# A transformer block on one core: the retention stage in rounds with inputs made a round ahead, decay carried by v, and three wide TensorE products per round whose result nothing reads

## The reference

```python
inner = jnp.einsum('bnihd,bnjhd->bnhij', qc, kc) * decay
inner = jnp.einsum('bnhij,bnjhe->bnihe', inner, vc)
def step(state, kv_chunk):
    k_i, v_i = kv_chunk
    new_state = (jnp.einsum('bjhd,bjhe->bhde', k_i * zeta[None, :, :, None], v_i)
                 + chunk_decay[None, :, None, None] * state)
    return new_state, state
cross = jnp.einsum('bnihd,nbhde->bnihe', qc, prev_states) * xi[None, None, :, :, None]
o = (inner + cross).reshape(b, s, h, dv)
mu = jnp.mean(o32, axis=-1, keepdims=True)
var = jnp.mean(jnp.square(o32 - mu), axis=-1, keepdims=True)
o = ((o32 - mu) * lax.rsqrt(var + RET_GN_EPS)).astype(dt).reshape(b, s, RET_WIDTH)
o = o * gn_w + gn_b
return jax.nn.silu(g) * o
```

## Time and profile before

| what | value |
|---|---|
| median of 3 runs | 2777.88 us (2776.36 to 2779.82) |
| profiled execution, its own time | 2776.76 us |
| its span, first to last instruction | 2775.0 us |
| PE, PEld, DVE, ACT, POOL busy | 94%, 80%, 56%, 40%, 37% of the span |
| mean granted TensorE clock | 0.950 of full speed |
| retention units, first to last `r_at`, layer 0 | 561.5 to 630.2 us |
| start of the output projection, layer 0 | 648.7 us |

### The profile page before, as it was taken

How to read it: one execution, slowest core, us unless ns; L and a number is a source line. 1 busy time by engine, 2 the same in 40 slices (tenths; PEclk the granted TensorE clock), 3 DMA queues, 4 the chain that set the end, 5 groups by cost and what they waited for, 6 DMA issues and landing times. The chain is left out here.

```text
span 2775.0 us, 43012 instructions
## 1 busy us (share of the span) xinstructions
PE 2597.4 (94%) x12940; PEld 2228.0 (80%) x12940; DVE 1560.8 (56%) x3033; ACT 1107.1 (40%) x2567; POOL 1039.7 (37%) x1229
## 2 busy tenths in 40 slices
PE   6999988889999999999989998988998999999997
PEld 5999877767778888888879998776776888888886
DVE  4666554473455445477656765544726544545785
ACT  4444543352532232244444455434515232322444
POOL 3455522183154544301034554222812555442012
PEclk9999999958999999999999999998599999999999
DMA  5111101121223332483331101012022323335633
GB/s 173 28 36 41 30 15 37 38 84 61 103 73 110 106 110 93 148 292 96 103 107 31 34 19 39 6 37 89 32 91 76 111 84 104 110 104 207 231 95 122
DMA packets 238651, 243.06 MB, mean 88 GB/s; under 512 B 27904, under 2 KB 170752, under 8 KB 238464
## 3 DMA queue, kind: packets, MB, share of 16 engines
q1 hardware_dynamic: 238464, 240.83, 27.0%
HBM read 173.14 MB, written 67.63 MB: 87 GB/s over the span
## 5 line engine op out<-in xcount | busy, mean ns | idle before, releaser
L2319 POOL TENSOR_TENSOR fw_a_lo<-fw_a_raw,fw_a_hi 128x512 fp32r<-128x512 f32 x132 | 178.7, 1354 | 520.6 <-DVE fw_s_raw L1913 520.6
L2319 POOL TENSOR_TENSOR fw_s_lo<-fw_s_raw,fw_s_hi 128x512 fp32r<-128x512 f32 x176 | 231.4, 1327 | 54.6 <-ACT fw_s_hi L1422 54.6
L718 PE MATMUL banks<-ht_hi,da_hi 128*128 128x512 f32 x496 | 192.9, 389 | 0.0
L718 PE MATMUL banks<-ht_lo,da_hi 128*128 128x512 f32 x496 | 192.9, 389 | 0.0
L718 PE MATMUL banks<-ht_hi,da_lo 128*128 128x512 f32 x496 | 192.9, 389 | 0.0
L718 PE MATMUL banks<-w_diff_hi,ht_hi 128*128 128x384 f32 x512 | 181.2, 354 | 6.3 <-DVE ht_lo L1609 4.3
L718 PE MATMUL banks<-w_diff_hi,ht_lo 128*128 128x384 f32 x512 | 172.9, 338 | 0.0
L718 PE MATMUL banks<-w_diff_lo,ht_hi 128*128 128x384 f32 x512 | 172.8, 337 | 0.0
L2158 POOL TENSOR_TENSOR qk_rot<-rope_a,rope_b 128x512 f32<-128x512 f32 x64 | 82.6, 1291 | 211.7 <-DVE rope_b L1638 211.7
L1666 DVE TENSOR_REDUCE stats<-banks 128x1 f32<-128x1024 f32 (+3 forms) x192 | 138.3, 747 | 29.8 <-PE banks L919 24.9
L718 PE MATMUL banks<-h_t_hi,fw_s_hi 128*128 128x512 f32 x352 | 139.9, 398 | 12.2 <-DVE h_t_lo L1917 8.2
(11 more groups left out here) (351 smaller groups left out, 7647.5 us busy)
## 6 DMA issues: line engine op xcount, KB each, us to landing
da_raw<-act_scratch SPq DMA_DIRECT2D x154, 256.0 KB, 2.7
fw_a_raw<-in_w_gate_dram SPq DMA_DIRECT2D x88, 256.0 KB, 3.0
act_scratch<-act_s SPq DMA_DIRECT2D x66, 256.0 KB, 3.0
w_diff_raw<-in_w_in_dram SPq DMA_DIRECT2D x24, 512.0 KB, 6.0
fw_a<-in_w_up_dram SPq DMA_DIRECT2D x44, 256.0 KB, 3.2
fw_a_raw<-in_w_up_dram SPq DMA_DIRECT2D x44, 256.0 KB, 2.9
act_scratch<-act_zero SPq DMA_DIRECT2D x44, 256.0 KB, 2.4
act_scratch<-act_one SPq DMA_DIRECT2D x44, 256.0 KB, 2.8
```

Of the source, the lines that this page charges most:

```text
L718: mm = pe.matmul(bank, lhsT, rhs, start=first and i == 0, stop=last and i == len(pairs) - 1, skip_group_check=resumes)
L2319: pool.tensor_tensor(w[1][:], w[2][:], w[0][:].bitcast(F32), ALU.subtract).then_inc(S["f_lo"], 1)
```

## The change

- The decays move onto v and the normalization. v is multiplied by gamma^-(j+1)/8 on VectorE right before its unit's rotation, in the MLA stage; `decay` becomes a 0/1 triangle (`causal`, 64 KB in place of 256 KB); the common factor left on a row drops out of the normalization, whose eps is scaled (`xz[:, p, 2:4]`). So `r_xzt`, its four scalings and the third transpose go. The state that is handed on is scaled by chunk decay where it is rounded.
- All engines loop over `RET_STEPS`, with v and the gate made two steps ahead. VectorE has the sum of the output first in a step (`ret_take`) and makes the rest of the state, which GpSimd made.
- The normalization moves from VectorE to ScalarE as scale and bias (`ret_normed`, with `ret_offset` on VectorE); root and finish on GpSimd take two units at once.
- `keep_clock` issues a product of 512 columns into a bank that nothing reads, after the transposes, after inner and after the output of every step: 48 per layer.
- The splits of the first half of the output weights stand in steps 4, 7, 10 and 13. `load_out(1)` waits for the finish of the fifth pair of units (`r_mx`, 5). The transposes of `mixed_rows` take the six column blocks of the attention heads first, of both halves of the rows, then the two of the retention.

```diff
-    xi = np.exp((pos[:, None] + 1.0) * log_gamma[None, :])
-    zeta = np.exp((P - 1.0 - pos)[:, None] * log_gamma[None, :]) * RET_DIM ** -0.5
+    age = (pos[:, None] + 1.0) * log_gamma[None, :].astype(np.float64)
     for p in range(RET_PAIRS):
-        c[:, C_XZ + 4 * p:C_XZ + 4 * p + 2] = xi[:, 2 * p:2 * p + 2]
-        c[:, C_XZ + 4 * p + 2:C_XZ + 4 * p + 4] = zeta[:, 2 * p:2 * p + 2]
...
+        RET_STEPS = range(RET_UNITS + 8)
+        ROUND_OUT = {4: 0, 7: 1, 10: 2, 13: 3}
...
-                arrives(decay[:], decay_dram.rearrange("p (a n) -> p a n", a=RET_PAIRS), "ret_in")
+                arrives(causal[:], causal_dram, "ret_in")
...
-                sp.wait_ge(S["r_xz"], L * PER["r_xz"] + T + 2)
-                sp.wait_ge(S["r_vlo"], L * PER["r_vlo"] + T + 2)
+                sp.wait_ge(S["r_mx"], L * PER["r_mx"] + T // 2 + 1)
                 sp.sem_inc(S["passed"], 1)
-                sp.wait_ge(S["tr_done"], L * PER["tr_done"] + RING - 2 * 2 * KD - RET_UNITS + T + 2)
                 load_out(1)
 
                 sp.wait_ge(S["x_saved"], L * PER["x_saved"] + 16)
                 sp.sem_inc(S["passed"], 1)
                 for half in range(2):
-                    sp.wait_ge(S["tr_done"], L * PER["tr_done"] + RING - NORM2_RINGS - 2 * KD + (half + 1) * KD)
+                    sp.wait_ge(S["tr_done"], L * PER["tr_done"] + RING - NORM2_RINGS - 2 + 2 * half)
...
+                def keep_clock():
+
+                    pe.matmul(banks[:, Z_BANK, :].rearrange("p (b n) -> p b n", b=4), ident_r[:],
+                              ident_r[:].unsqueeze(1).to_broadcast([P, 4, P]), start=True, stop=True)
+
                 def ret_transpose(p, t):
                     n = p * T + t
-                    pe.wait_ge(S["r_xz"], L * PER["r_xz"] + n + 1)
+                    pe.wait_ge(S["rope_sum"], L * PER["rope_sum"] + ROPE_RET + n + 1)
                     bank = take_ring()
                     pe.transpose(bank[:, tokens(0)], r_rot[n][:, 0:2, :].rearrange("p a d -> p (a d)"), ident[:])
-                    pe.transpose(bank[:, tokens(1)], r_rot[n][:, 2:4, :].rearrange("p a d -> p (a d)"), ident[:])
-                    pe.transpose(bank[:, tokens(2)], r_xzt[n % 3][:, 0:2, :].rearrange("p a d -> p (a d)"), ident[:])\
-                        .then_inc(S["tr_done"], 1)
+                    pe.transpose(bank[:, tokens(1)], r_rot[n][:, 2:4, :].rearrange("p a d -> p (a d)"), ident[:]).then_inc(S["tr_done"], 1)
                     ret_ready[n] = ring[0]
 
                 ret_ready = {}
...
-                for n in range(1, RET_UNITS + 3):
-                    if n <= RET_UNITS:
-                        ret_transpose((n - 1) // T, (n - 1) % T)
-                    if 2 <= n < RET_UNITS + 2:
-                        ret_inner((n - 2) // T, (n - 2) % T)
-                    if n >= 3:
-                        ret_output((n - 3) // T, (n - 3) % T)
-
-
                 pe.wait_ge(S["z_free"], L * PER["z_free"] + Z_UNITS)
+                for u in RET_STEPS:
+                    if u < RET_UNITS:
+                        ret_transpose(u // T, u % T)
+                        keep_clock()
+                    if 0 <= u - 1 < RET_UNITS:
+                        ret_inner((u - 1) // T, (u - 1) % T)
+                        keep_clock()
+                    if 0 <= u - 2 < RET_UNITS:
+                        ret_output((u - 2) // T, (u - 2) % T)
+                        keep_clock()
+
+
                 ring_empty()
                 pe.wait_ge(S["mix_in"], L * PER["mix_in"] + 16)
-                transpose_rows(mixed_rows[:, 0:4, :], "r_mx", T + 4)
-                transpose_rows(mixed_rows[:, 4:8, :], "r_mx", 2 * T)
+                for blocks in (range(KD - 2), range(KD - 2, KD)):
+                    for half in range(2):
+                        if blocks[0]:
+                            pe.wait_ge(S["r_mx"], L * PER["r_mx"] + T // 2 + 2 * half + 2)
+                        transpose_rows(mixed_rows[:, 4 * half:4 * half + 4, :], "mix_in", 16, blocks)
...
-                def ret_scaled(n):
-
+                    act.activation(r_z[n][:, 3 * P:4 * P], r_z[n][:, 3 * P:4 * P], ACT.Silu).then_inc(S["r_gate"], 1)
+
+                def ret_high_k(n):
                     act.wait_ge(S["rope_sum"], L * PER["rope_sum"] + ROPE_RET + n + 1)
-                    if n >= 3:
-                        act.wait_ge(S["tr_done"], L * PER["tr_done"] + ret_ring + n - 2)
-                        act.wait_ge(S["r_kzlo"], L * PER["r_kzlo"] + n - 2)
-                    for i in range(4):
-                        st = act.activation(r_xzt[n % 3][:, i, :], r_rot[n][:, i, :], ACT.Copy, scale=xz[:, n // T, i:i + 1])
-                    st.then_inc(S["r_xz"], 1)
-
-                ret_ring = RING - NORM2_RINGS - 2 * KD - 2 * T
...
+                def ret_normed(n):
+                    m, i = n // 2, n % 2
+                    b = m % 2
+                    act.wait_ge(S["r_nb"], L * PER["r_nb"] + m + 1)
+                    if m >= 2:
+                        act.wait_ge(S["r_mx"], L * PER["r_mx"] + m - 1)
+                    for j in range(2):
+                        st = act.activation(r_norm[b][:, i, 64 * j:64 * j + 64], r_sum[m % 3][:, i, j, :], ACT.Identity,
+                                            bias=r_nb[:, b, 2 * i + j:2 * i + j + 1], scale=r_rs[:, b, 2 * i + j:2 * i + j + 1])
+                    st.then_inc(S["r_on"], 1)
...
-                for n in range(1, RET_UNITS + 2):
-                    if 1 <= n <= RET_UNITS:
-                        ret_high_k(n - 1)
-                        ret_high(n - 1)
-                    if n >= 2:
-                        ret_inner(n - 2)
-                    if n + 1 < RET_UNITS:
-                        ret_gate_and_v(n + 1)
-                        ret_scaled(n + 1)
-                    if 2 <= n < 2 + PARTS:
-                        weights(CH_OUT, [n - 2])
+
+                for u in RET_STEPS:
+                    if u < RET_UNITS:
+                        ret_high(u)
+                        ret_high_k(u)
+                    if u + 2 < RET_UNITS:
+                        ret_gate_and_v(u + 2)
+                    if 0 <= u - 7 < RET_UNITS:
+                        ret_normed(u - 7)
+                    if 0 <= u - 1 < RET_UNITS:
+                        ret_inner(u - 1)
+                    if u in ROUND_OUT:
+                        weights(CH_OUT, [ROUND_OUT[u]])
                 weights(CH_OUT + 1)
-                high_rows(0, None)
-                high_rows(1, None)
+                for blocks in (range(KD - 2), range(KD - 2, KD)):
+                    for half in range(2):
+                        high_rows(half, None, blocks)
...
+                    v = r_z[n][:, 2 * P:3 * P].rearrange("p (j d) -> p j d", j=2)
+                    dve.tensor_tensor(v, v, xz[:, n // T, 0:2].unsqueeze(2).to_broadcast([P, 2, RET_DIM]), ALU.mult)
                     rotate(r_z[n][:, 0:2 * P], r_ab[0], r_ab[1], n % T).then_inc(S["rope_ab"], 1)
...
+                def ret_take(n):
+                    m, i = n // 2, n % 2
+                    dve.wait_ge(S["ro_done"], L * PER["ro_done"] + n + 1)
+                    if m >= 3:
+                        dve.wait_ge(S["r_on"], L * PER["r_on"] + 2 * (m - 2))
+                    dve.tensor_reduce(r_sum[m % 3][:, i], banks[:, RET_OUT[0]:RET_OUT[1] + 1, 0:P].rearrange("p j (c d) -> p j d c", c=2),
+                                      AX_X, ALU.add).then_inc(S["r_take"], 1)
...
+                def ret_state_low(n):
+                    p = n // T
+                    if n % T < T - 1:
+                        i = rs_count(n)
+                        dve.wait_ge(S["r_sthi"], L * PER["r_sthi"] + i + 1)
+                        dve.scalar_tensor_tensor(r_st2[i % 3][:, 1, :], r_st[:], cd[:, p:p + 1], r_st2[i % 3][:, 0, :].bitcast(F32),
+                                                 ALU.mult, ALU.subtract).then_inc(S["r_stlo"], 1)
+
+                def ret_offset(m):
+                    b = m % 2
+                    dve.wait_ge(S["r_rstd"], L * PER["r_rstd"] + m + 1)
+                    if m >= 2:
+                        dve.wait_ge(S["r_on"], L * PER["r_on"] + 2 * (m - 1))
+                    dve.scalar_tensor_tensor(r_nb[:, b, :], mv[:, b, :, 0], -1.0, r_rs[:, b, :], ALU.mult, ALU.mult).then_inc(S["r_nb"], 1)
...
-                for n in range(1, RET_UNITS + 4):
-                    if 1 <= n <= RET_UNITS:
-                        ret_low(n - 1)
-                    if 2 <= n < RET_UNITS + 2:
-                        ret_inner(n - 2)
-                    if n >= 4:
-                        ret_normed(n - 4)
-                    if n + 1 < RET_UNITS:
-                        ret_low_v(n + 1)
-                    if 3 <= n < RET_UNITS + 3:
-                        ret_moments(n - 3)
+                for u in RET_STEPS:
+                    if 0 <= u - 3 < RET_UNITS:
+                        ret_take(u - 3)
+                    if u < RET_UNITS:
```

(56 more changed lines are left out.)

106 lines of the change are left out of this document (39 added, 67 removed).

## The result

The changed kernel takes 2813.96 us (median of 4 runs, 2810.99 to 2817.09); the kernel before took 2777.12 us beside it. Ratio 1.0133, interval 1.0116 to 1.0151: slower by 1.3%. The forecast was 2811, its range 2781 to 2826.

The account below looks back on a forecast made before the run. The retention stage was taken as bound by the larger of GpSimd's unit and TensorE's low-clock step. Per layer 7.0 + 9.3 + 0.5 = 16.8 us, twice 33.6, on 2777.9 gave 2811.5, stated as 2811; range 2781 to 2826.

Parts of the forecast that it names:

- The clock: Retention stage, both layers: TensorE's clock stays low (1.2 GHz, 0.50) despite three wide products per step; forecast's chance 0.62.
- Step 1: Retention stage: one transpose goes, three wide products come; a full step takes 5.47 us, +7.0 us per layer.
- Step 2: Tail from last `r_at` to projection: output-weight load now waits for the fifth pair's finish; 27.9 against 18.6 us, +9.3 per layer.
- Step 3: GpSimd in the retention stage: unit falls to 2.8 from 4.15 us, but this gains nothing at a step of 5.5.
- Step 4: VectorE between the MLA heads: 16 operations multiply v by a decay; 0 to 6 us, taken as 0.5 per layer.
- The early clock: Rival in the retention stage: clock rises in the first steps and holds, GpSimd then bounds; 2751 us, chance 0.15.
- the hidden tail: Rival: retention steps are slower, but the tail stays hidden by an early fifth-pair finish or short load; 2793 us, chance 0.07.
- the free wide products: Rival in the retention stage: wide products fill TensorE's slack at no cost, only the tail is lost; 2797 us, chance 0.05.

Follow-up runs that it names:

- the kernel with nine: The changed kernel with nine wide products per step in place of three: 2787.7 us, ratio 1.0040 against the kernel before.
- the burst kernel: The changed kernel with twelve more wide products in one run ahead of the second inner, still three per step: 2767.8 us, ratio 0.9970 against the kernel before.

## Why the prediction was right, and where its steps were off

**The clock.** Right: 0.50 through the stage in both layers. The forecast's reason, that three wide products among narrow ones are nearer to the mix that stays low, is borne out by the kernel with nine, which rises, and by the changed one, which doesn't. "Busy all the time" was too much for the stage before (63.89 of 71 us), but holds in the changed kernel. What the forecast missed is that with the same three a clock that is already up stays up for 33 us or more. Part 1 of the Trainium skill's "TensorE: Matmul & The Clock Gate" has it that "activity releases the throttle". By that rule, with busy time read as activity, the stage would have run at 1.00; busy for 77.85 of 79 us at 0.50, the trace does not agree.

**Step 1, the stage.** Forecast 5.47 us a step and +7.0; measured 5.73 and +8.9. The removed transpose was right (4.56 - 0.21 = 4.35, measured without wide products). The mis-sized term is the wide product: 0.42 from a row of wide products only, and 0.14 a step taken off for a gap that one of them would cover; in this mix it is 0.46 net for each, with nothing to take off.

**Step 2, the tail.** The size was nearly right (27.9 forecast, 29.3 measured). The chain up to the load's landing was right to 0.2 us (4.5 + 9.1 = 13.6 forecast; 5.7 + 7.7 = 13.4), and the roundings are 3.9. What was too small is the rest: from the first `ht_hi` to the projection are 668.35 - 656.35 = 12.0 us, not 9.65 + 0.7. TensorE's transposes come at 0.50 for the groups from 658.9 to 663.1, and ScalarE's `ht_hi` 0.85 us apart, which the forecast had only as a bound. What it had wrong is the price of the load: it took 9.1 us as all on the path, and to take 4.9 of them away is worth 1.2. Beside the load runs the retention's own end; the forecast followed it only to the fifth pair. The last three finishes of two units each come one after another on GpSimd, ScalarE's last `r_norm` waits for the first of them, and the last `mixed_rows` is 5.6 us later behind the last `r_at` than before. With the load out of the way this takes its place. That the two chains end within 0.94 us of each other, so that a sum along one of them gave the tail, was luck.

**Step 3, GpSimd.** Nothing in this kernel, right, as 5.7 us of TensorE cover it. But the forecast wrote that TensorE's step was the longer one in the kernel before; several steps there were GpSimd's. With the cover gone the relief is worth up to 10.2 - 15 x 0.21 = 7 us a layer, an estimate from the kernel without wide products, in which the other changes of order stand as well.

**Step 4**, v times decay, wasn't tested by itself, so its 0.5 is not shown. Stage and tail give 19.6 a layer and the spans 18.9, so nothing is missing that it would have to fill.

**The rivals.** The early clock was put at 2751 and 0.15: the burst kernel shows that it can be had, 2768 with the clock up for some 33 of 56 us; it needs another 12 products in a wait, which the change hasn't. Two rivals, the hidden tail (2793) and the free wide products (2797), lay inside the stated range too, so the time alone does not speak for the forecast. What decides against them is the tail of 29.3 us, and the 34 us that the kernel without wide products gains.

## What to carry to other kernels

Price products that are only there for the clock against having none. Three in each step at the low clock cost their own length and lifted nothing (34 us); a run of twelve in a wait and three per step brought 46 us against the changed kernel, but only 12 against the same kernel without any (2767.8 against 2780.2), and 4 to 6, within noise, once the tail was mended. When a wait is put on a late event, look at what runs to the same point beside it before you give it the whole price: take it away alone, and the next one stands there. Read which engine sets each step, not the mean step: a stage can have two bounds by turns.

## What was not expected of the hardware

What the clock is in this stage depends on where it stood before. The same work per step runs at 1.00 for 20 us when it starts high, and at 0.50 for 22 us, busy without a pause in both, when it starts low. A step of three wide products is 3.29 us at the full clock and 5.73 at half, a factor of 1.74 and not 2; six more wide ones cost 4.68 - 3.29 = 1.39 us at the full clock, 0.23 each, half of the 0.46 at the low one, so it is the narrow ones that gain less (4.35 against an estimated 3.29 - 3 x 0.23 = 2.60, a factor of 1.67).
